# Combining four experts' terms at a time instead of two, in the first quarter of a product-key expert layer

## The reference, cut to what matters

```
sub_scores = jnp.einsum('thpd,hpkd->thpk', query, sub_keys)
half_vals, half_idx = lax.top_k(sub_scores, PEER_TOPK)            # 16 of 128, twice
cand = half_vals[:, :, 0, :, None] + half_vals[:, :, 1, None, :]
top_vals, top_pos = lax.top_k(cand, PEER_TOPK)                    # 16 of 256
experts = i1 * PEER_N_KEYS + i2
gates = jax.nn.softmax(top_vals, axis=-1)

u = expert_down[eb]                                               # 512 tokens x 8 heads x 16 rows of 1024
act = jax.nn.gelu(jnp.einsum('td,thkd->thk', xb, u)) * gb
vv = expert_up[eb]
return jnp.einsum('thk,thkd->td', act, vv)
```

## Time and profile before

| | us |
|---|---|
| median of three runs | 3034.7 |
| the profiled execution, its own time | 3024.2 |
| its span | 3022.4 |
| PE busy | 2280.7 (75%) |
| DVE busy | 1422.7 (47%) |
| ACT busy | 757.0 (25%) |
| POOL busy | 595.2 (20%) |

### The profile page before, as it was taken

One profiled execution on the slowest core, in us unless ns is written; L12 is line 12 of the kernel. 1 busy time (PEld: TensorE's weight loads), 2 busy tenths in 40 slices (PEclk: granted clock), 3 DMA queues, 4 the chain that ended last, 5 costly groups with the idle time before them and its releaser, 6 DMA issues. The chain is left out here.

```text
span 3022.4 us, 28783 instructions
## 1 busy us (share of the span) xinstructions
PE 2280.7 (75%) x9732; PEld 960.1 (32%) x9732; DVE 1422.7 (47%) x3332; ACT 757.0 (25%) x1748; POOL 595.2 (20%) x587
## 2 busy tenths in 40 slices
PE   5997899887787874899779998777665665565554
PEld 2543444532222221455656443222211111111110
DVE  2576310510000003101258657657777777777765
ACT  2104310110010001312158663322222222232222
POOL 0000000010000001000012222344444434444442
PEclk9999999899898986989789889898887868777777
DMA  9178339399999995321047867899999999999996
GB/s 333 59 258 286 141 101 240 146 359 404 398 400 404 403 402 199 132 84 72 29 167 264 326 256 284 346 417 414 415 421 421 421 421 422 421 411 421 421 421 265
DMA packets 213260, 922.17 MB, mean 305 GB/s; under 512 B 18986, under 2 KB 58968, under 8 KB 121230
## 3 DMA queue, kind: packets, MB, share of 16 engines
q0 software_dynamic: 78864, 552.72, 45.0%
q1 hardware_dynamic: 124480, 359.15, 32.3%
q10 hardware_dynamic: 9790, 8.73, 0.9%
HBM read 888.78 MB, written 31.77 MB: 305 GB/s over the span
## 5 line engine op out<-in xcount | busy, mean ns | idle before, releaser
L2510 PE MATMUL bank<-ring,arena_w 128*32 128x512 f32 x1568 | 603.8, 786 | 317.1 <-ACT arena_w L1279 316.8
L865 POOL DMA_INDIRECT ring<-in_expert_pair,ids x392 | 424.4, 1083 | 1095.6 <-PE bank L2510 678.9
L1905 PE MATMUL bank<-arena_h,ring 128*128 128x512 f32 (+1 forms) x1008 | 363.9, 522 | 2.4 <-ACT arena_h L1013 1.4
L2185 PE MATMUL bank<-ring,arena_h 128*64 128x512 f32 x1056 | 275.6, 681 | 86.1 <-DMA ring<-in_w_exp_up 77.0
L2510 PEld LDWEIGHTS bank<-ring,arena_w 128*32 128x32 f32 x1568 | 104.4, 128 | 658.9 <-ACT arena_w L1279 472.3
L1854 DVE CUSTOM_DVE_ANT_0 ring<-ring,arena_h 128x1024 f32<-128x1024 f32 x203 | 245.3, 1225 | 83.5 <-DMA ring<-in_expert_pair,ids 50.3
L1854 DVE CUSTOM_DVE_ANT_0 ring<-ring 128x1024 f32<-128x1024 f32 x189 | 229.8, 1225 | 79.4 <-DMA ring<-in_expert_pair,ids 71.0
L1277 ACT ACTIVATE arena_w<-arena_w 128x2 f32<-128x2 f32 x256 | 51.9, 203 | 776.0 <-DVE arena_w L1854 775.6
L1599 DVE TENSOR_TENSOR arena_q<-arena_q,bank 128x256 f32<-128x256 f32 x32 | 13.5, 422 | 481.6 <-ACT arena_q L1040 481.6
L1905 PEld LDWEIGHTS bank<-arena_h,ring 128*128 128x128 f32 x1008 | 175.0, 196 | 181.0 <-issue 177.8
L2185 PEld LDWEIGHTS bank<-ring,arena_h 128*64 128x64 f32 x1056 | 91.7, 158 | 267.6 <-issue 257.9
(11 more groups left out here) (468 smaller groups left out, 3009.2 us busy)
## 6 DMA issues: line engine op xcount, KB each, us to landing
ring<-in_w_exp_gate SPq DMA_DIRECT2D x33, 2048.0 KB, 20.2
ring<-in_w_exp_up SPq DMA_DIRECT2D x33, 2048.0 KB, 24.7
ring<-in_w_exp_down SPq DMA_DIRECT2D x33, 2048.0 KB, 25.6
ring<-in_w_in SPq DMA_DIRECT2D x15, 2048.0 KB, 19.8
ring<-in_w_mod SPq DMA_DIRECT2D x12, 2048.0 KB, 19.4
ring<-in_w_ada SPq DMA_DIRECT2D x12, 2048.0 KB, 14.9
xs_d<-zeros SPq DMA_DIRECT2D x1, 12032.0 KB, 69.8
ys_d<-arena_h ACTq DMA_DIRECT2D x64, 128.0 KB, 7.2
```

The lines of the kernel that those rows point to most:

```text
L865: pool.indirect_dma_start(pair[pair_of(m)], None, A["expert_pair_2"], bass.IndirectOffsetOnAxis(ap=ids[n % 2][:, r:r + 1], axis=0)).then_i ...
L1905: mm = pe.matmul(dst, w[:, c, at], rhs[:, c, :], start=(c == 0), stop=(c == chunks - 1))
L2185: mm = pe.matmul(bank[2 + b][at, :].rearrange("p (g f) -> p g f", g=2), xbT[b][:, c, :], gu[:, :, c, 256 * half:256 * half + 256], start=( ...
L2510: mm = pe.matmul(bank[4 + 2 * (n // H % 2) + half][at, :], sel_q[:, n % 2, k0 + j, :], pair[pair_of(m + j)][:, D + 512 * half:D + 512 * ha ...
```

## The change

For rounds 0 to 7 the terms are combined four at a time instead of two. ACT waits for four dot products in parts 1, 3, 5 and 7, takes gelu of all four, and scales four selection matrices; in the even parts it has no such work. The table for exp and log is then loaded only in the odd parts. PE adds four terms in parts 2, 4 and 6 and the round's last four at the beginning of the next round. Rounds 8 to 31 stay as they are. DVE and POOL run the same instructions in the same order.

```diff
-                coefs(n, 2 * part, 2)
-                if n < H and PLAN[n][part]:
+                if n >= H:
+                    coefs(n, 2 * part, 2)
+                elif part % 2 == 1:
+                    coefs(n, 2 * part - 2, 4)
                     if any(s < ST_FOX for parts in PLAN[n:] for steps in parts for s in steps):
                         act.preload_act_table_set(EXP_LN)
...
-                if part >= 1:
-                    up_sums(n, 2 * part - 2, 2)
+                if n >= H:
+                    if part >= 1:
+                        up_sums(n, 2 * part - 2, 2)
+                elif part in (2, 4, 6):
+                    up_sums(n, 2 * part - 4, 4)
...
-                if n > 0:
+                if n > H:
                     up_sums(n - 1, K16 - 2, 2)
+                elif n > 0:
+                    up_sums(n - 1, K16 - 4, 4)
```

## The result

The changed kernel is slower: 3058.3 us (median of 8 runs, 3048.6 to 3068.6) against 3027.7 (8 runs, 3018.0 to 3036.8). The ratio is 1.0096, 95% interval 1.007 to 1.012, so +29 us where -7 was forecast. Its profiled execution was one of its quicker ones: span 3038.0, against 3022.4 before.

The account below looks back on a forecast made before the run. Bounds: no engine free in rounds 0 and 1, PE in 2 and 3, projections, norms and buffers in 4 and 5, transfers from round 6. Sum -8 - 18 + 11 + 8 = -7 against 3024.2: 3017 us, range 3004 to 3052.

Parts of the forecast that it names:

- Rounds 2 and 3, -18: Rounds 2 and 3: PE is the bound, seven calls of 2.5 us fewer give -18 us, ends -29 and -7.
- the prediction's own condition: Rounds 2 and 3: the forecast counts as wrong if they gain under 10 us.
- Rounds 0 and 1, -8: Rounds 0 and 1: lighter ACT and PE shorten DVE's waits, -8 us, ends -11.4 and +3.
- 11.4 us of waits: Rounds 0 and 1: DVE's waits of 4.7 + 3.6 + 3.1 us, the most it could give back.
- Rounds 4 and 5, +11: Rounds 4 and 5: buffers released behind the projections make gathers late, +11 us, ends +5 and +15.
- the late 4/9: Round 4: gather 4/9, its buffer released behind the output projection, lands 10.6 us late; DVE waits some 9 us.
- Rounds 6 and 7, +8: Rounds 6 and 7: slower buffer reuse and a release behind the query projection cost +8 us, ends +3 and +14.
- 7/4 to 7/7: Gathers early in round 7: buffers released behind round 6's query projection make 7/4 late, +4 us.
- the turn to round 8: End of round 7: the same late release, mostly covered by three additional buffers, +2 us.
- the way round of the groups of four: Rounds 6 and 7: buffer reuse from last landing to next takes 10.9 or 12.6 us against 12.45; 2 us for eight groups.
- rival 2: Rounds 4 to 7: the way round through 8 buffers decides, +31 there, -15 in rounds 0 to 3; +16, 3051; chance 0.15.
- Rival 1: Rounds 0 to 7: late gathers cost little, gains at larger values, -22 us, 3013; chance 0.30.

Follow-up runs that it names:

- e2: The kernel before with terms by fours in rounds 2 and 3 only: ratio 0.9997 (0.9975 to 1.0018) to the kernel before.
- e17: Second profile of the kernel before with fours in rounds 2 and 3 only: those two rounds lasted 152.7 us.
- e15: Second profile of the changed kernel, nothing edited: span 3068.6 us.
- e9: The kernel before with fours in rounds 2 and 3 only, TensorE's calls in parts 2, 4 and 6 one attention step later: ratio 1.0024 to the kernel before.
- e1: The kernel before with fours in rounds 0 and 1 only: ratio 1.0003 (0.9982 to 1.0024) to the kernel before.
- e3: The kernel before with fours in rounds 4 and 5 only: ratio 1.0024 to the kernel before, +7 us.
- e11: The changed kernel without fours in round 4: ratio 1.0074 to the kernel before, 7 us under the whole change.
- e8: The changed kernel plus 24 TensorE matmuls adding zero in rounds 6 and 7: ratio 1.0095 to the kernel before.
- e7: The kernel before with fours in rounds 4 to 7 only: ratio 1.0079 to the kernel before, +24 us.

## Why the prediction was wrong, step by step

**Rounds 2 and 3, -18: this is the step that failed.** It took seven calls of 2.5 us off a PE that is the bound, at an unchanged clock of 0.82. In round 2 the calls went and PE was the bound, but the price of a us of work was not fixed: 10 us less of full-clock work, and the same length on average. By the times the two rounds gave 0 (e2), by the profiles -11.1 and +6.8. By the first profile alone the prediction's own condition, a gain of at least 10 us, would have been met; that was luck. In the second profile of the changed kernel, within round 2:

```profile
1693.00:1696.00 3.00, 3.00 (x11) 1.98 (x12) 0.19 (x1) 0.00 (x0) 1.88 (x2) 0.81 0.99 397
1696.00:1699.00 3.00, 3.00 (x8) 1.15 (x6) 1.19 (x5) 0.56 (x2) 1.88 (x2) 0.76 1.07 411
1699.00:1711.00 12.00, 12.00 (x32) 3.91 (x30) 9.23 (x28) 6.13 (x14) 0.42 (x1) 0.50 1.02 410
1711.00:1723.00 12.00, 12.00 (x31) 6.75 (x30) 3.86 (x8) 1.76 (x4) 3.33 (x4) 0.50 1.03 415
1723.00:1727.00 4.00, 4.00 (x18) 3.20 (x22) 2.72 (x12) 3.71 (x7) 0.00 (x0) 0.50 0.44 178
```

28 us at half clock without a pause, and the clock fell at about 1698, when PE had been busy without a pause since 1687.3 (behind a wait of 5.0 us for ScalarE) and had just come to full clock. In e17 a wait stood ahead of such a stretch:

```profile
1703.00:1709.00 6.00, 6.00 (x32) 3.75 (x31) 3.44 (x8) 1.46 (x5) 1.87 (x2) 1.00 0.96 393
1709.00:1711.00 2.00, 0.14 (x2) 0.00 (x0) 1.56 (x6) 1.96 (x5) 0.00 (x0) 0.83 0.97 406
1711.00:1739.00 28.00, 27.63 (x86) 14.24 (x90) 14.53 (x36) 12.01 (x29) 3.74 (x4) 0.50 0.46 183
```

The wait is new: PE stands at the call for four until ACT has scaled the four matrices (2.2 to 2.6 us, three such in rounds 2 and 3 of e2, 7.0 us in all; before there was 0.2). In the first profile of the changed kernel the same wait of 2.2 us was followed by full clock (the call behind it took 1.9 us), so it alone doesn't decide. The Trainium skill (TensorE: Matmul & The Clock Gate, Part 1) ties half rate to an idle array; e17 looks like that, e15's 28 us with PE busy throughout do not. What sets the clock in such a stretch is open. In round 3 the clock fell too in all seven profiles in which ACT and PE both go by fours as in the change: 0.74 to 0.77 for 0.82, and the round lasted 76.2 to 77.4 us, where it was 73.7 to 74.1 by twos. That is +2.7, with 6 us less full-clock work. There PE was not the bound throughout: it was idle for 13.3 us of the round before and for 18.0 and 18.7 in the two profiles of the changed kernel, so the new waits count there as well as the clock. e9 moved these waits and did not remove them, so how much of the loss is theirs is open.

**Rounds 0 and 1, -8.** Came at 0 (e1); in the profiles 121.0 to 122.1 us with fours and 118.1 to 121.7 without. DVE was rightly named as the limit, but of its 11.4 us of waits only the 4.7 for ACT were ACT's to give. 3.1 of them went, and other waits came: in all DVE waited 15.2 us in the first profile and 14.1 in the second (and 14.1 in e2, where these rounds are unchanged). I expected later gathers to be covered; in the second profile DVE waited 3.0 us for them, and in the first 6.0:

```profile
DVE ring L1856 <- DMA ring<-in_expert_pair,ids: 6.0, 3, 4.5
```

ACT's 14 loads less (18 us; 16 were forecast) and PE's 13 us of full-clock work less bought nothing that the runs show.

**Rounds 4 and 5, +11.** Right: +12.3 in the profile, +7 us in e3's times, the late 4/9 at 11.0 for 10.6 and a wait of 9.3 us for the forecast 9. e11 takes it away again. The kernel before is at the short end here: unchanged, the two rounds lasted 112.7 to 117.9 us in ten profiles, and by fours 124.4 to 125.1 in six, so the cost is between 6.5 and 12.4.

**Rounds 6 and 7, +8.** The mechanism was right, the size short: +12.7 and +12.0. In the first profile the 12.7 is made of steps between dots that grew: 3.7 us over 7/4 to 7/7 (4 were forecast) and 1.5 at the turn to round 8 (2 were forecast), both as said; and then 2.5 at 6/1, 2.7 over 6/8 and 6/9, 1.2 over 7/0 and 7/1 and 2.5 at 7/12, less 1.3 that came back between. So the mis-sized term is the way round of the groups of four: 2 us in all were written, and it measured 7.5. I had set a way round of 10.9 or 12.6 us against 12.45, which holds only if POOL's issues and the transfers fit without slack; rival 2 had named that. In the second profile the same places gave less and 7/4 more (4.7 over 7/4 to 7/7). The clock was 0.54 (the forecast had "under 0.74" as the sign of rival 2), but e8 shows at most 2.9 us that could be its part, and e7 has the same length without more clock.

**The rivals.** Rival 2 (slower, 3051) had the right sign, and the place for rounds 4 to 7: +24.9 and +24.1 against its +31. It still gave rounds 0 to 3 -15, and they gave none. Rival 1 took DVE's 36 us of waiting in rounds 2 and 3 as a sign of gain; the times gave none of it.

The sum made of what was measured: about 0 for rounds 0 to 3 by e1 and e2, and +24 for rounds 4 to 7 by e7. That leaves 5 us of the 29 unplaced, which is within the intervals. Of the 36 us between forecast and result 26 are the gain that rounds 0 to 3 did not give, 5 are rounds 4 to 7.

## What to carry to other kernels

Merging calls on an engine that waits for others delays what the calls release; count the buffers it holds against the longest block of work that stands between two releases, since that is where it costs. Saved work on TensorE is worth its share of the time only if the granted clock stays: weigh busy time x clock, not busy time, and don't book a gain until two profiles agree on the clock. Before taking load off an engine, look whether the engine that sets the end waits for it; here 18 us less of table loads in rounds 0 and 1 gave no time.

## What the hardware showed that I had not expected

Unchanged code had a granted clock of 0.81 to 0.92 in the same round, and lasted 66.0 to 75.8 us, in five kernels that don't differ in that round; four of them don't differ in anything that runs before round 4. TensorE ran 28 us at half clock while it was busy without a gap. And adding matmuls of zeros to a round that TensorE bounds, some 6 us of full-clock work by busy time x clock, went with a round that was 7 us shorter (68.4 and 68.2 us for 76.1 and 75.4), while in the next round some 10 us of them went with 9 us more (86.3 and 86.8 for 77.4 and 77.3).
